# Halving the first modulation block and moving one query head into the compressed-key chunk

## The reference

```
sh1, sc1, g1, sh2, sc2, g2 = split(silu(cond) @ w_mod + b_mod, 6)     # w_mod: 2048 x 12288
h  = rms_norm(x, g_attn) * (1 + sc1) + sh1
z  = h @ w_in                                    # a_q a_k a_v | b_q b_k b_v | c_q (4x192) | c_kv (256) | c_kr (64)
c:  ckv_n = rms_norm(c_kv, c_kvn);  kv = ckv_n @ w_ukv;  k = rms_norm([k_nope, c_kr], c_kn);  q = rms_norm(c_q, c_qn)
o  = concat(attention_a, attention_b, attention_c) @ w_o;   x = x + g1 * o
x  = x + g2 * moe(rms_norm(x, g_ffn) * (1 + sc2) + sh2)              # 32 experts, top 2
```

## Time and profile before

| | us |
|---|---|
| median of three runs | 1692.18 |
| profiled execution, first to last instruction | 1691.8 |
| TensorE busy | 1591.9 |
| VectorE busy | 690.1 |
| ScalarE busy | 263.7 |
| GpSimd busy | 106.1 |

### The profile page before, as it was taken

The page is one execution under the profiler, slowest core; times in us unless marked ns, Lnnn a source line. Parts: engine busy times, 40 slices in busy tenths (PEclk is TensorE's granted clock), DMA queues, the critical chain, the costliest instruction groups (busy, mean ns, idle before and its releaser), DMA issues.

```text
span 1691.8 us, 18209 instructions
## 1 busy us (share of the span) xinstructions
PE 1591.9 (94%) x6671; PEld 655.4 (39%) x6716; DVE 690.1 (41%) x1361; ACT 263.7 (16%) x706; POOL 106.1 (6%) x192
## 2 busy tenths in 40 slices
PE   5999999999999999999999998999999999998998
PEld 3455555544434444443332332333233233233332
DVE  3113232113245893344444345345344433544444
ACT  2004221112133000011101101110110111111010
POOL 1022100100020100000000000000000000000000
PEclk9999999999999999999999999999999999999999
DMA  9992643535199765599999999999999999999995
GB/s 394 420 385 120 230 193 119 215 109 213 54 368 410 275 264 221 203 366 426 427 429 428 428 425 428 428 424 428 427 426 428 425 424 427 428 428 423 428 427 237
DMA packets 60526, 581.94 MB, mean 344 GB/s; under 512 B 9129, under 2 KB 10121, under 8 KB 16105
## 3 DMA queue, kind: packets, MB, share of 16 engines
q1 hardware_dynamic: 53120, 557.34, 79.6%
q0 software_dynamic: 6064, 23.22, 3.6%
q10 hardware_dynamic: 1296, 0.77, 0.2%
HBM read 584.06 MB, written 7.05 MB: 349 GB/s over the span
## 4 chain that ended last, share of the span: by engine, by line
PE 68%; DMA 17%; DVE 4%; issue 2%; ACT 1%; SPq 0%; POOL 0%; ACTq 0%
PE bank L1298 24%; DMA ring<-in_w 17%; PE bank L1046 14%; PE bank L1208 7%; PE bank L1025 7%; DVE r L1794 2%; PE bank L920 2%; PE bank L1331 2%; PE bank L1133 2%; PE bank L1257 2%; PE bank L1280 1%; PE bank L1108 1%; PE bank L1194 1%; PE bank L1116 1%; PE bank L1313 1%
## 5 line engine op out<-in xcount | busy, mean ns | idle before, releaser
L1298 PE MATMUL bank<-ring,r 128*64 128x512 f32 x1920 | 469.6, 619 | 45.5 <-DMA ring<-in_w 45.5
L1298 PEld LDWEIGHTS bank<-ring,r 128*64 128x64 f32 x1920 | 129.6, 140 | 303.3 <-issue 303.3
L1046 PE MATMUL bank<-ring,r 128*128 128x384 f32 (+1 forms) x672 | 242.4, 519 | 0.0
L2014 DVE TENSOR_TENSOR bank<-bank,r 128x512 f32<-128x512 f32 x180 | 125.9, 700 | 266.2 <-PE bank L1208 266.2
L1331 PE MATMUL bank<-ring,mod_row 128*64 128x512 f32 x896 | 195.4, 593 | 7.9 <-ACT mod_row L1547 7.9
L1025 PE MATMUL bank<-ring,r 128*128 128x512 f32 x384 | 170.0, 595 | 0.0
L1046 PEld LDWEIGHTS bank<-ring,r 128*128 128x128 f32 x672 | 126.9, 191 | 103.7 <-issue 44.7
L1208 PE MATMUL bank<-r 128*128 128x512 bf16 x495 | 137.6, 382 | 7.2 <-issue 7.2
L2016 DVE TENSOR_TENSOR r<-r,bank 128x512 f32<-128x512 f32 x180 | 123.7, 687 | 6.2
L1331 PEld LDWEIGHTS bank<-ring,mod_row 128*64 128x64 f32 x896 | 75.4, 137 | 118.2 <-issue 107.9
L1208 PEld LDWEIGHTS bank<-r 128*128 128x128 bf16 x540 | 38.0, 97 | 167.4 <-DVE r L2016 97.4
(11 more groups left out here) (281 smaller groups left out, 1238.4 us busy)
## 6 DMA issues: line engine op xcount, KB each, us to landing
ring<-in_w SPq DMA_DIRECT2D x180, 2048.0 KB, 17.8
ring<-in_w_mod SPq DMA_DIRECT2D x64, 1024.0 KB, 11.8
ring<-in_w_first SPq DMA_DIRECT2D x32, 1024.0 KB, 25.9
ring<-in_w SPq DMA_DIRECT2D x19, 1024.0 KB, 9.7
ring<-in_w_o SPq DMA_DIRECT2D x16, 1024.0 KB, 6.2
r<-mod_d POOLq DMA_DIRECT2D x8, 1024.0 KB, 8.0
ring<-in_w_aq SPq DMA_DIRECT2D x8, 768.0 KB, 11.4
ring<-in_w_bq SPq DMA_DIRECT2D x8, 768.0 KB, 13.0
```

The source lines that it names most:

```text
L1046: mm = pe.matmul(acc[acc_of(a)][:, 0:w], h_t[:, k, t * P:(t + 1) * P], wu[:, j, :], start=(k == 0), stop=(k == KD - 1))
L1298: mm = pe.matmul(ps[64 * c:64 * c + 64, :], xg_t[:, j, 64 * c:64 * c + 64], big_cut(slot_of(u), (8, 512))[:, j % 8, :], start=(j == 0), st ...
L2014: v.tensor_tensor(ps[:, :], ps[:, :], g2b[:, min(t, 1), cols], ALU.mult).then_inc(strip_scaled, 1)
```

## The change

There are three edits. The blocks of the first modulation become five: two of 256 columns with two units for each half, and three of 512 as before. A unit of the small blocks holds eight row groups of 256 columns. The order of the start changes with it: two tiles are transposed ahead of the first unit. The chunk `ckv` becomes 512 wide: one head of `c_q` (192 columns), `c_kv` and `c_kr`. The chunk `cq1` becomes 192 wide, one head. And `cq1`, `cq0` and `aq0` are now taken tile by tile together, with attention C starting in `aq1`.

```diff
-CHUNKS = [("ckv", CKV, 320), ("cq0", Q_C, 384), ("cq1", Q_C + 384, 384),
+CHUNKS = [("ckv", Q_C + 576, 512), ("cq0", Q_C, 384), ("cq1", Q_C + 384, 192),
+BLOCKS = ((0, 256, 2), (256, 256, 2), (512, 512, 4), (1024, 512, 4), (1536, 512, 4))
+EARLY_AFTER = {0: 0, 2: 1, 3: 2, 4: 3}
...
+    chunk_units("cq1")
+    for t in range(TILES):
+        job("proj", ("cq1", t))
+        if t == 0:
+            units.append(("ukv",))
+            steps.append(("cache", "c"))
+            kvc(0, 0)
+            kvc(0, 1)
+            chunk_units("aq0")
+        else:
+            mods(3)
+        job("proj", ("cq0", t))
+        kvc(t + 1, 0)
+        kvc(t + 1, 1)
+        job("proj", ("aq0", t))
...
+                if m == 0 and b:
+                    pe.wait_ge(modt_ready, 2 * b + c - 1)
+                for q in range(rows):
+                    g = 32 * (q % 4)
+                    mm = pe.matmul(ps[g:g + 3, 0:width], csil[:, rows * m + q, :], w[:, q, :],
+                                   start=(m == 0 and q < 4), stop=(m == n_units - 1 and q >= rows - 4))
...
             turn_xn(0)
+            turn_xn(1)
             pe.wait_ge(csil_ready, 2)
             pe.wait_ge(cleared, 1)
             first_unit(0, 0, 0)
-            turn_xn(1)
+            turn_xn(2)
             first_unit(0, 0, 1)
-            turn_xn(2)
-            first_unit(0, 0, 2)
-            first_unit(0, 0, 3)
             first_turn(0, 0)
...
+            early_block(range(0, 2), 1, ((0,), (1,), (2,), (3,)), (2, 3))
+            early_block(range(2, 4), 2, ((0, 1), (2, 3), (4, 5), (6, 7)), (2, 3))
+            for i in (1, 2):
+                early_block(range(4 * i, 4 * i + 4), i + 2, ((0, 1), (2, 3), (4,), (5,), (6,), (7,), (), ()), (3, 6))
+            early_block(range(12, KD), len(BLOCKS), (), ())
...
+                    elif kind == "cq1":
+                        cols = [0, 384]
+                    elif kind == "ckv":
+                        cols = [192, 320, 0, 384]
...
-                        e.activation(junk[:, 256:320], ps[:, 256:320], ACT.Square, accum_out=kr_ss[:, kt:kt + 1])
-                        e.activation(kr[:, kt, :], ps[:, 256:320], ACT.Copy)
-                        last = e.activation(z[:, 0:256], ps[:, 0:256], ACT.Copy)
+                        e.activation(junk[:, 192:448], ps[:, 192:448], ACT.Square, accum_out=ss[n % 3][:, 1:2])
+                        e.activation(junk[:, 448:512], ps[:, 448:512], ACT.Square, accum_out=kr_ss[:, kt:kt + 1])
+                        e.activation(kr[:, kt, :], ps[:, 448:512], ACT.Copy)
+                        last = e.activation(z[:, 0:448], ps[:, 0:448], ACT.Copy)
```

More of the change, by code:

```diff
@@ L176, in mod @@
         steps.append(("mod", g, k))
-    for i in range(4):
-        units.extend(("first", g, i, m) for g in FIRST_GROUPS for m in range(4))
+    for b, (_, _, n_units) in enumerate(BLOCKS):
+        units.extend(("first", g, b, m) for g in FIRST_GROUPS for m in range(n_units))
     later = [(g, k) for g in LATER_GROUPS for k in range(KD)]
@@ L237, in plan, with chunk_units @@
         job("proj", ("ckv", t))
+    def chunk_units(name):
+        units.extend([("in", name, i) for i in range(4)])
+    chunk_units("cq1")
[13 more added lines that the diff above has]
+        job("proj", ("aq0", t))
     for name, _, _ in CHUNKS:
-        if name in EARLY:
+        if name in EARLY + ("cq1", "aq0"):
             continue
-        units.extend([("in", name, i) for i in range(4)])
+        chunk_units(name)
         for t in range(TILES):
-            attends = (name == "aq0" and t > 0) or (name == "aq1" and t < 2) or name in ("bq1", "bkv")
+            attends = name in ("aq1", "bq1", "bkv") or (name, t) == ("bq0", 0)
             job("proj", (name, t), norm=not attends)
             n = len(jobs) - 1
[L246 to L258, removed]
+            mods(2 if attends and (name, t) != ("bkv", 2) else 0)
             if name == "akv" and t == 0:
                 steps.append(("cache", "a"))
[L261 to L264, removed]
+            if name == "aq1":
+                attend("C", [t])
+            if (name, t) == ("bq0", 0):
+                attend("C", [TILES], flush=True, drain=(0, 1, 1, 1))
             if name == "bq1":
@@ L681, in build @@
         uses = [0] * SLOTS
-        for u in range(unit_no[("first", FIRST_GROUPS[1], 3, 3)] + 1):
+        for u in range(unit_no[("first", FIRST_GROUPS[1], len(BLOCKS) - 1, 3)] + 1):
             if u not in frees:
@@ L833, in arrived, with first_unit, first_turn @@
                 pe.wait_ge(*full_of(m))
-            def first_unit(i, c, m):
-                u = unit_no[("first", FIRST_GROUPS[c], i, m)]
+            def first_unit(b, c, m):
+                _, width, n_units = BLOCKS[b]
+                u = unit_no[("first", FIRST_GROUPS[c], b, m)]
                 arrived(u)
[L840 to L853, removed]
+                ps, rows = first_ps[c], KD // n_units
+                w = cut(ring_slot(u), (rows, width))
+                if m == 0 and b:
[4 more added lines that the diff above has]
+                                   start=(m == 0 and q < 4), stop=(m == n_units - 1 and q >= rows - 4))
+                mm.then_inc(*((slot_free[ring_slot(u)], 1) if m < n_units - 1 else (first_full, 1)))
+            def first_turn(b, c):
+                pe.wait_ge(first_copied, 2 * b + c + 1)
+                for x in range(BLOCKS[b][1] // P):
+                    mm = pe.matmul(first_ps[c][:, 3 * x:3 * x + 3], first_row[c][:, x * P:(x + 1) * P], K("fold"),
                                    start=True, stop=True)
@@ L1655, in _ @@
             hmod(0)
-            for i in range(1, 4):
+            for i in range(1, len(BLOCKS)):
                 for c in range(2):
```

143 lines of the change are left out of this document (83 added, 60 removed).

## The result

The changed kernel takes 1701.99 us (median of 4 runs, 1701.66 to 1702.64) beside 1692.31 us for the kernel before on the same chip. The ratio is 1.0058, 95% interval 1.0045 to 1.007: slower by 9.7 us where 8.6 had been forecast. The profiled span is 1700.2 us, 8.4 more than before.

What follows compares the result with a forecast made beforehand. TensorE's passage through the first two stages was taken to set the time, the byte-bound expert stage carrying any shift whole. Terms summed to +8.6 us on a 1691.8 us span, plus 0.4: 1700.8 us; 8 in 10 within 1691 to 1708.

Steps and rivals of the forecast that it cites:

- start, to the early end: Up to TensorE's end of the last early part: sooner early parts traded against bare handovers and small units, +1.0 us.
- waits behind `cq1` tile 2: Three mod steps behind cq1 tile 2 wait for ring transfers issued late: +4.0 us, bounds 1.5 and 6.
- lower clock behind them: After the mod waits TensorE works at a lower clock, sized from one slow projection: +1.0 us, bounds 0 to 1.75.
- first turn: Behind the early parts, ckv tile 0's longer chain of copies and scalings delays its turn: +0.5 us.
- ScalarE's state outputs: At cq1 tile 0 ScalarE's copy must wait for two output transfers: +1.5 us, bounds 0 and 4.5.
- each further one takes 2.5 more: Ring behind cq1 tile 2: after a lone 1 MB transfer's 5.1 us, each further one lands 2.5 us later.
- I expect 5.4 to 6.5: Landing time in us of the output transfers that ScalarE's cq1 tile 0 copy awaits, engines being quiet by then.
- one `ckv` turn that waits for ScalarE: Sign expected in the trace after: a ckv turn on TensorE held up by ScalarE.
- Double records: Rival at the start: small units cost double, +6.6 us over the forecast's term, 1707.4 us; chance 0.05.
- The cold array: Rival at the start: without a unit before, first unit and tile 2 run at half pace, 1703.6 us; chance 0.13.
- Start wins, back waits little: Rival: ScalarE terms vanish, handovers cost 1.2 each: 1696.2 us, or 1693.7 with small ring waits; chance 0.18.
- Faster: Rival: from tile 1 TensorE is bound by work alone, waits behind it under 2.3 us, 1686.5 us; chance 0.10.

Runs made afterwards that it cites:

- e12: Kernel before with the new widths alone (ckv 512, cq1 192), whole blocks and the old chunk-by-chunk order: 1694.91 us, ratio 1.0018.
- e4: Changed kernel with the plan of before (chunk by chunk), half blocks and new widths kept: 1694.79 us, ratio 1.0019.
- e2: Changed kernel with the three mod steps of tile 2 between the kvc jobs and aq0 tile 2: 1697.1 us, ratio 1.0027.
- e3: Changed kernel with four whole blocks of 512 and the old start; new widths and tile-by-tile order kept: 1701.76 us, ratio 1.0051.
- e5: Changed kernel, but SyncE issues the first unit of aq1 only when the last lone mod unit has landed: 1706.01 us, ratio 1.0071.
- e7: Changed kernel with the first small unit between the transposes of tiles 0 and 1: 1700.34 us, ratio 1.0039.
- e8: Changed kernel with units of blocks 1 and 2 one early part sooner, one part behind each block's last turn: 1699.37 us, ratio 1.0034.
- e1: Changed kernel with the three mod steps of tile 2 behind aq0 tile 2: 1698.0 us, ratio 1.0031.
- e9: Kernel before with the halved first modulation block and its start alone: 1696.5 us, ratio 1.0024.
- e6: Kernel before with the four units of aq0 ahead of the first three mod units in the ring; cq1 stays 384 wide: 1693.25 us, ratio 1.0002.
- e10: Kernel before with the halved block and its start (e9), plus the edits of e7 and e8: 1692.84 us, ratio 1.0004.
- e11: Changed kernel with the edits of e2, e7 and e8 together: 1692.75 us, ratio 1.0001.

## Why the prediction was right

Right in direction, nearly in size (1700.8 forecast, 1702.0 measured), and in the cause. By the runs: widths alone +2.4 (e12), half blocks on top -0.1 (e4), the order on top +7.2 (the kernel after). Of these 7.2, 4.9 go when three "mod" steps move one job back (e2), and in the trace 6.85 of 8.5 in the middle. Term by term, from the trace up to the first tile of `akv`:

| term | forecast | measured |
|---|---|---|
| narrow passes | +0.3 | +0.2 (5.20 us for 32 records: 163 ns each) |
| transposes | +0.3 | +0.3 |
| start, to the early end | +1.0 | -0.9 |
| waits behind `cq1` tile 2 | +4.0 | +5.4 (4.5 to 5.8 in e3, e5, e7 and e8) |
| lower clock behind them | +1.0 (0 to 1.75) | +2.7 |
| first turn | +0.5 | +0.7 |
| ScalarE's state outputs | +1.5 | -0.1 |
| sum | +8.6 | +8.3 of 8.7 |

**The start.** Its parts came as forecast: 29.94 us for 29.8, no weight waits, two bare handovers of 1.5 and 1.9 (3.4 for 4.0). Small units cost no surcharge, so the 0.8 was wrong. The handovers inside the first block got 0.6 shorter (0.62 + 0.55 for 0.89 + 0.82), which the sum left out. But the size is not a constant. The same start ran in six profiled kernels (after, e1, e2, e4, e5, e9), and its early end, without the moved work, is 127.3 to 132.0 us, mean 129.9. The four with the old start (before, e3, e6, e12) give 127.6 to 129.2, mean 128.3. What differs within each set is mainly how much runs at the lower pace: tile 1 and the first unit take 3.12 + 1.51 us in the kernel after and 3.67 + 1.89 in e9, and later stretches come or don't. In the runs the halving costs 4.0 alone (e9), nothing on the new widths (e4 less e12: -0.1; after less e3: +0.2). That it doesn't add is shown. The windows from 10.3 us to the early end tell which part of it doesn't. TensorE's idle time there is 7.7 and 9.4 us without and with half blocks on the old widths (before, e9), 7.3 and 9.1 (e12, e4) and 7.6 and 8.9 (e3, after) on the new ones: the halving costs 1.3 to 1.8 us of idle time everywhere. Its busy time rises by 2.1 us on the old widths (110.2 to 112.3) and falls by 1.3 and 2.1 on the new ones (125.3 to 124.0, 125.5 to 123.5). Each pair does the same columns of work, so that is the pace, and these are single traces. Whether wide parts keep it up or chance does stays open.

**The ring.** The mechanism was right and two sizes were low. The step "each further one takes 2.5 more" failed: issued within 2.9 us, the three units were used 3.4 us apart. I first blamed the unit of `aq1` behind them, and e5 refuted that. Most parts of a unit do come 2.5 to 2.7 us after those of the one ahead (e5), but TensorE waits for the last part. With the issues 2.6 us apart no part is late (e6: the 16 parts of the third unit within 0.3 us). The lower clock was sized from one slow projection. Here it lasted from the third wait through the third unit, a turn and one `kvc` job, outside the bound. That both hang on one cause is shown by e2, where both are gone, and by e6, where the same slots with a tile of double length give neither (0.16 us of wait at most).

**ScalarE.** The step "I expect 5.4 to 6.5" failed: the output landed in 1.7 us (6.8 before, with weights in flight), so the wait of TensorE there didn't grow (1.17 for 1.28 before). The sign "one `ckv` turn that waits for ScalarE" showed as a wait of 0.73 us for VectorE, which stands behind ScalarE in that chain. This miss and the two low ones nearly cancel, so the sum is better than its terms.

**The rivals.** *Double records* fell: 0.96 us a unit. *The cold array* fell for the most part: the first unit lost 0.5 us, not 1.0, and tile 2 ran at full pace. In e7 a unit ran at full pace (1.04) with nothing ahead of it but 16 transposes, so transposes alone can be followed by the higher clock. In e12 the first 16 transposes themselves took 3.26 us, not 3.65, and the unit behind them 1.04. That speaks against the rule of the Trainium skill ("TensorE: Matmul & The Clock Gate", Part 4: PE-mode transpose) that transposes don't count as busy time for the clock. But it isn't reliable: in e10 and e11 a unit at the same place took 1.89. *Start wins, back waits little* was right on ScalarE and wrong on the ring. *Faster* fell: the waits left behind tile 1 come to 13.0 us up to the ring's, as counted, not under 2.3.

No version beats the kernel before. The mended one (1.0001) and half blocks with cover (1.0004) are level with it.

## What to carry to other kernels

Where weights come through a ring in a fixed order, a unit's transfer starts when the work on the unit 12 places before it frees its slot. So shortening one tile can stall a later step that the diff doesn't touch: for each unit, set the time from that release to its use against a landing time, whenever widths or order change. Cover every handover to another engine with one piece of ready work behind it. A sooner start is worth only what the slowest stream lets through, here the weights.

## What the runs showed of the hardware

- In all 14 traces, by windows of the granted clock, each stretch at the lower clock costs 1.7, 3.4 or 5.1 us, the one that the end of the span cuts off aside. Most follow waits of TensorE of 0.7 to 3.4 us in the five traces in which the rows ahead of them were read (at 842 us before: 2.54 for `ring<-in_w`), but not every such wait has one, and they shift between kernels whose code up to there is the same. The runs of one kernel spread by up to 7 us (e4: 1692.6 to 1699.7), so a single trace can't size an edit of 2 us here.
- A 128 KB output landed in 1.7 us with quiet DMA engines, and in 6.8 us with weights in flight.
- Three lone 1 MB transfers issued within 2.9 us were ready for use 3.4 and 3.9 us apart, with no other weights beside them (e5), and 2.5 to 3.5 us apart in the four other kernels with these waits. In e5, 13 of 16 parts landed 2.5 and 2.7 us apart from unit to unit, and the last part up to 2.0 us behind them. Issued 2.6 us apart, such transfers took 4.7 us each (e6).
